# Splitting w_down in three stages instead of two: a new spread of 64 pieces, with ScalarE issuing the output projection's stores

## The chip, the cores and the metric

The kernel runs on one NeuronCore of one Trainium2 chip. The metric is the device time of one execution in microseconds (us); lower is better. The engines are TensorE (PE in the profile, its weight loads PEld), VectorE (DVE), ScalarE (ACT), GpSimd (POOL) and SyncE (SP, which here only issues DMAs). SP and ScalarE each have a queue of DMAs of their own.

## What is computed

One layer of a hybrid decoder on 2048 prompt tokens and 8 sample tokens, width 1024, all float32:

```
proj = x @ w_in                        # columns: u (512), v (512), xs (512)
u = gelu(proj_u);  v = layer_norm(gelu(proj_v))
y_a = u * chunk_spatial_gate(v)        # 128x128 lower-triangular W_s per head, chunks of 128 tokens
y_b, state = s5_mixer(xs)              # diagonal complex state space layer, 32 groups, then gelu and GLU
x1 = layer_norm(2**0.25 * x + concat(y_a, y_b) @ w_out)
y  = layer_norm(2**0.25 * x1 + grouped_moe(x1))     # 16 experts, top 2; h @ w_down[e] per expert
```

TensorE multiplies rounded fp32r operands. To keep float32 accuracy each operand is split in a high part (rounded to fp32r) and a low part (the difference), and a product is made of three: high x high, high x low, low x high.

## The kernel before

The program is five stages with a barrier of all engines behind each (`phase()`). In the time of the profiled execution:

* **Input projection**, 0 to 270 us. 8 halves `i` of 256 tokens, 4 feature groups `f` each; a step is `n = 4 i + f`. TensorE turns the rows of x, and projects them to xs and u (L697). ScalarE rounds the turned x (`high`, L404), VectorE makes its low part (`low`, L478). From step `LATE` = 16 on, each step also builds the matrices of one pair of state groups: VectorE computes them (`v_pair`, L632 to L635), TensorE turns them (`pair_mats`, L715, L724), VectorE copies them out (`results`, L642). VectorE's order in a late step is `v_pair`, `xs_tile` (L491), `low` in even steps, `results`. ScalarE's is `u_tile` (L416), then `high` in even steps. GpSimd builds other matrices beside it (L373 to L389).
* **v projection**, 270 to 391 us. 16 tiles `c` of 128 tokens. TensorE multiplies (L1087; the gate's product L1065 for tile c - 3), ScalarE applies gelu (L920), VectorE normalises tile c + 4 and gates tile c (`norm_tile`, `gate_tile`) and fills cosine and sine tables between them (`table_step`); at c = 6 it also does the sample tokens. The turned x comes back from DRAM in 8 parts of two tiles, in two buffers: `half(i)` on SP's queue (L862) once the product of tile 2 i - 3 is done. At the end SP issues the first loads of the next stage (L805 to L807) when the tables are finished (`tables_set`, L1050).
* **State space layer**, 391 to 519 us.
* **Output projection**, 519 to 789 us. 17 tiles `p` (tile 0 is the sample). ScalarE rounds the mixer's output of tile p + 2 (`high`, L1655), GpSimd makes the low part (`low`, L1591) and behind it, in its own order, the inverse root for the layer norm of tile p (`root`, L1596); TensorE multiplies (L1831), turns x1 (L1842) and does the router's product (L1851). VectorE's order is `norm(p + 1)`, `turn(p)`, `units(p)`, and every second tile `select` (the experts' choice, L1717 on). Its `norm` needs GpSimd's root (L1776), so ScalarE's `high` stands ahead of it.
* **Experts**, 789 to 1352 us.

**The split of w_down.** w_down is 64 pieces of 128 x 512 ("units"). Each is loaded from the input to SBUF, ScalarE writes its high part, VectorE its low part, and both parts are stored to DRAM, 256 KB each, from where the experts' stage loads them. This rides along with other stages. Before, 24 units are split in the input projection and 40 in the output projection. In the input projection the list `UNITS` gives step and place of each unit: SP loads at step n (L298), ScalarE rounds at n + 1 behind `u_tile` and ahead of `high` (L420), VectorE subtracts at n + 2 (L495), SP stores at n + 3 (L291). In the output projection `STEPS_D[p]` has the units of tile p. SP loads them behind the layer norm of tile p (L1559), ScalarE rounds them in `units(p)` (L1688) at the end of tile p and thus ahead of its `high(p + 3)`, VectorE subtracts them (L1791), and SP stores them in its turn for tile p + 1 (`units_out`, L1565), behind the loads and stores of that tile. There SP may load the units of tile p only when the stores of tile p - 2 have landed.

Of the kernel before, what the change touches and what calls it, by code (L numbers as in the profile page):

```python
# [6 lines left out]
P = 128  # L7
# [23 lines left out]
SUP = 512  # L31
# [66 lines left out]
def hybrid_step(nc, a, o):  # L98
    ctx = ExitStack()
    with ctx, nc.allow_non_contiguous_dma(reason="small parameters are laid out by state"):  # L100
# [93 lines left out]
        with phase() as ph:  # L194
# [22 lines left out]
            LIFE = 4  # L217
            UNITS, busy = [], {}
            for n in range(6, 27):
                free = [s for s in SLOTS if busy.get(s, 0) <= n and n + LIFE <= SLOTS[s]]  # L220
                free.sort(key=lambda s: SLOTS[s])
                for s in free[:1 + n % 2]:
                    if len(UNITS) < 24:
                        UNITS.append((n, s))
                        busy[s] = n + LIFE
            AUNITS = len(UNITS)
            assert AUNITS == 24, AUNITS
            wd_ld, wd_st = ({s: phase_sem(f"wd_{k}_{s}") for s in SLOTS} for k in ("in", "stored"))
            wd_high, wd_low = sems("a_wd_high a_wd_low")

            def units_at(n):
                return [(j, s, sum(u[1] == s for u in UNITS[:j])) for j, (m, s) in enumerate(UNITS) if m == n]

# [19 lines left out]
            def _(sp):  # L253
# [33 lines left out]
                def units(n):  # L287
                    for j, s, m in units_at(n - 3):
                        sp.wait_ge(wd_low, j + 1)
                        for h in range(2):  # L290
                            sp.dma_start(wd_dram[h][j // 4, :, j % 4 * SUP:(j % 4 + 1) * SUP],  # L291
                                         wd_part(s, 1 - h, True).bitcast(F32)).then_inc(wd_st[s], 16)
                    for j, s, m in units_at(n):
                        if m:
                            sp.wait_ge(wd_st[s], m * 32)
                        elif s[0] == "x":
                            sp.wait_ge(turned[int(s[1])], 1)
                        sp.dma_start(wd_part(s, 0, False), wd_src[j // 4, :, j % 4]).then_inc(wd_ld[s], 16)  # L298
# [97 lines left out]
            def _(act):  # L396
# [15 lines left out]
                def u_tile(i, f):  # L412
                    act.wait_ge(u_prod, i * FT + f + 1)
                    if f == 0 and f"y{i}" in SLOTS:
                        act.wait_ge(wd_st[f"y{i}"], uses(f"y{i}") * 32)
                    nc.scalar.activation(ya[:, 2 * i:2 * i + 2, f, :], pu[f % 2][:, 0:XH].rearrange("p (t n) -> p t n", n=P),  # L416
                                         ACT.Gelu_apprx_tanh).then_inc(u_out, 1)
                    for j, s, m in units_at(i * FT + f - 1):
                        act.wait_ge(wd_ld[s], m * 16 + 16)
                        nc.scalar.copy(wd_part(s, 1, True), wd_part(s, 0, False)).then_inc(wd_high, 1)  # L420
# [47 lines left out]
            def _(dve):  # L468
# [18 lines left out]
                def xs_tile(i, f):  # L487
                    dve.wait_ge(xs_prod, i * FT + f + 1)
                    if i % 2 == 0 and i:
                        dve.wait_ge(ust_stored[f], i // 2 * 16)  # L490
                    v.tensor_copy(ust[:, f, :, i % 2 * (KS // 2):(i % 2 + 1) * (KS // 2)].rearrange("p j k -> p k j"),  # L491
                                  pxs[f % 2][:, 0:XH].rearrange("p (k j) -> p k j", j=L)).then_inc(xs_out, 1)
                    for j, s, m in units_at(i * FT + f - 2):
                        dve.wait_ge(wd_high, j + 1)
                        v.tensor_tensor(wd_part(s, 0, True), wd_part(s, 0, False), wd_part(s, 1, True).bitcast(F32),  # L495
                                        ALU.subtract).then_inc(wd_low, 1)
# [312 lines left out]
        with phase() as ph:  # L809
# [44 lines left out]
            LAG = 3  # L854
            SMP = 10
            block = ph.enter_context(nc.Block())

            @block.sync
            def _(sp):
# [18 lines left out]
                for j in range(L):  # L878
                    sp.dma_start(toep[:, j, :], k_dram[(L - 1 - j) * Q:(L - 1 - j) * Q + P, :]).then_inc(toep_in, 16)
                for i in range(2, NH):  # L880
                    sp.wait_ge(v_prod, 2 * i - 2)
                    half(i)
                sp.wait_ge(vs_set, 1)
# [31 lines left out]
            def _(act):  # L915
# [12 lines left out]
                nc.scalar.activation(vs[:], psv[:, :], ACT.Gelu_apprx_tanh).then_inc(vs_gelu, 1)  # L928
                with act.Fori(1, CH // 4 - 1) as i:
                    for b in range(4):  # L930
                        gelu(i * 4 + b, b, False)
                for b in range(4):
                    gelu(CH - 4 + b, b, False)

            @block.vector
            def _(dve):
# [106 lines left out]
                for c in range(CH - 4):  # L1043
                    gate_tile(c, c % 4)
                    if c < len(rest):
                        table_step(*rest[c])
                    norm_tile(c + 4, c % 4)
                    if c + 4 == SMP:
                        sample()
                v.memset(tw[:, 3], 0.0).then_inc(tables_set, 1)  # L1050
                for c in range(CH - 4, CH):
# [411 lines left out]
        with phase() as ph:  # L1463
# [40 lines left out]
            wd_high, wd_low = sems("d_wd_high d_wd_low")  # L1504
            STEPS_D, used, left = {}, {}, NUNITS - AUNITS
            for p in range(2, CH):
                free = [t for t in range(p) if used.get(t, 0) <= p - 2][:min(3 + (p in (8, 12)), left)]
                STEPS_D[p] = [(NUNITS - left + k, t) for k, t in enumerate(free)]
# [17 lines left out]
            def _(sp):  # L1526
# [33 lines left out]

                def units_out(p):
                    sp.wait_ge(wd_low, landed(p, 1, 1))
                    for u, t in STEPS_D[p]:
                        for h in range(2):
                            sp.dma_start(wd_dram[h][u // 4, :, u % 4 * SUP:(u % 4 + 1) * SUP],  # L1565
                                         (yb_r, ya_r)[h][:, t].bitcast(F32)).then_inc(wd_st[p % 2], 16)

                for p in range(2, CH + 1):
# [5 lines left out]
                    stores(p, p % 2)  # L1574
                    if p - 1 in STEPS_D:
                        units_out(p - 1)
                for b in range(2):
                    sp.wait_ge(wd_st[b], landed(CH - 2 + b, 2, 32))
                for s in (x1_stored, ax1_stored):
# [69 lines left out]
            def _(act):  # L1649
# [33 lines left out]
                act.wait_ge(sc_zero, 1)  # L1683
                score(0, NS)
                def units(p):
                    act.wait_ge(wd_ld[p % 2], landed(p, 2, 16))
                    for u, t in STEPS_D[p]:
# [13 lines left out]
            def _(dve):  # L1701
# [83 lines left out]
                for k in range(KD):  # L1785
                    dve.wait_ge(wo_high, k + 1)
                    v.tensor_tensor(wo[1][:, k, :], w_out[:, k, :], wo[0][:, k, :].bitcast(F32), ALU.subtract).then_inc(wo_low, 1)
                def units(p):
                    dve.wait_ge(wd_high, landed(p, 1, 1))
                    for u, t in STEPS_D[p]:  # L1790
# [23 lines left out]
                turn(CH - 1, 1)  # L1814
                units(CH - 1)
                norm(CH, 0, False, CH // 2)
# [644 lines left out]
```

## Time and profile before

| | |
|---|---|
| time, median of 3 runs | 1350.77 us (1349.82 to 1352.14) |
| the profiled execution | 1353.23 us, span 1351.6 us |
| TensorE busy | 1193.4 us, 88% |
| VectorE busy | 924.0 us, 68% |
| ScalarE busy | 513.0 us, 38% |
| GpSimd busy | 479.3 us, 35% |
| DMA | 290 MB, mean 215 GB/s |
| granted TensorE clock, mean | 0.943 of full speed |

The span is from the first to the last instruction; the execution's own time is 1.6 us more. The busy shares are averages over stages with different limits, so each stage has to be read by itself: which engine works without a pause in it, and which wait ends last. Of a busy time only the part that nothing else covers is in the total.

### The profile page before, as it was taken

Reading aid. Unit: us, or ns where it says so; the run is one execution under the profiler, and the core shown is the slowest. Engines: PE = TensorE matmul, PEld = TensorE weight load, DVE = VectorE, ACT = ScalarE, POOL = GpSimd, SP = SyncE. Lnnn points to the kernel's source line nnn. Section 1 sums busy time; section 2 is a strip of 40 time slices with the busy share of each in tenths; the row PEclk is TensorE's granted clock in tenths of the full one; section 3 lists DMA queues with packets and bytes.
Section 4 is the critical chain, followed back from the end, with each engine's and each line's share of the span. In section 5 each row is a group of like instructions: output and inputs, shape, how many; then the busy total and the mean of one; then the engine's idle time right before and its main releaser. Section 6 shows DMA issues by size and latency. Waiting matters only on the chain. (4 is left out here: it accounts for less than half of the span.)

```text
span 1351.6 us, 23750 instructions
## 1 busy us (share of the span) xinstructions
PE 1193.4 (88%) x7005; PEld 1014.3 (75%) x7006; DVE 924.0 (68%) x2044; ACT 513.0 (38%) x808; POOL 479.3 (35%) x552
## 2 busy tenths in 40 slices
PE   7999889799978977999999668999999999999910
PEld 6997889778867744888887567888888888888800
DVE  3463875558877745457777686877787778777685
ACT  4131111100003254223223224666666666666533
POOL 3108860100010003322222023555554555454467
PEclk9999899999989988999989778999999999999965
DMA  8589684674335332457877774899989889745594
GB/s 257 166 311 289 190 267 136 180 222 170 126 104 160 116 130 57 155 187 262 270 268 256 257 288 165 265 288 317 278 274 297 246 255 303 218 95 121 123 348 171
DMA packets 142833, 290.04 MB, mean 215 GB/s; under 512 B 54632, under 2 KB 71608, under 8 KB 131472
## 3 DMA queue, kind: packets, MB, share of 16 engines
q1 hardware_dynamic: 126320, 231.99, 50.2%
q0 software_dynamic: 15408, 55.12, 17.4%
q10 hardware_dynamic: 1040, 2.10, 0.5%
q8 instruction: 37, 0.61, 0.2%
q14 instruction: 28, 0.23, 0.1%
HBM read 177.90 MB, written 111.13 MB: 214 GB/s over the span
## 5 line engine op out<-in xcount | busy, mean ns | idle before, releaser
L2174 DVE TENSOR_TENSOR wgu<-w_raw,wgu (+1 forms) x192 | 229.9, 1220 | 83.4 <-ACT wgu L2270 82.6
L2391 PE MATMUL p_gu<-wgu,xg_high 128*128 x768 | 246.4, 402 | 8.3 <-DVE xg_low L2167 4.5
L2270 ACT CAST wgu<-w_raw x188 | 192.6, 1051 | 55.3 <-issue 52.3
L2391 PEld LDWEIGHTS p_gu<-wgu,xg_high 128*128 128x128 f32 x768 | 141.4, 190 | 42.4 <-issue 15.1
L2391 PE MATMUL p_gu<-wgu,xg_low 128*128 x384 | 152.0, 396 | 0.0
L2053 POOL TENSOR_TENSOR spare_e<-nothing 128x1 f32<-128x1 f32 x48 | 46.4, 966 | 219.0 <-DVE yo L2193 219.0
L2054 POOL DMA_INDIRECT acc_rows<-yo,si x48 | 112.3, 2340 | 8.7 <-issue 8.7
L1831 PE MATMUL p_out<-w_out_high,mixt_high 128*128 128x512 f32 x256 | 103.4, 404 | 0.0
L1831 PE MATMUL p_out<-w_out_high,mixt_low 128*128 128x512 f32 x256 | 101.5, 396 | 0.0
L1831 PE MATMUL p_out<-w_out_low,mixt_high 128*128 128x512 f32 x256 | 101.3, 396 | 0.0
L2391 PEld LDWEIGHTS p_gu<-wgu,xg_low 128*128 128x128 f32 x384 | 72.8, 190 | 15.8
L2415 PE MATMUL p_d<-wd_high,ht_high 128*128 x192 | 80.1, 417 | 1.3 <-DVE ht_low L2187 1.3
L697 PE MATMUL pxs<-xt_high,w_xs_high 128*128 128x256 f32 x256 | 77.7, 303 | 2.7 <-DVE xt_low L478 2.0
L1591 POOL TENSOR_TENSOR mixt_low<-ya,mixt_high 128x512 fp32r<-128x512 f32 x16 | 22.8, 1426 | 155.2 <-ACT mixt_high L1655 155.2
L2415 PE MATMUL p_d<-wd_high,ht_low 128*128 x192 | 75.9, 395 | 0.0
L2415 PE MATMUL p_d<-wd_low,ht_high 128*128 x192 | 75.7, 394 | 0.0
L697 PE MATMUL pxs<-xt_high,w_xs_low 128*128 128x256 f32 x256 | 75.1, 294 | 0.0
L697 PE MATMUL pxs<-xt_low,w_xs_high 128*128 128x256 f32 x256 | 75.1, 293 | 0.0
L2167 DVE TENSOR_TENSOR xg_low<-p_xt,xg_high 128x512 fp32r<-128x512 f32 x96 | 61.8, 685 | 16.4 <-ACT xg_high L2257 15.8
L697 PE MATMUL pu<-xt_high,w_u_high 128*128 128x256 f32 x256 | 72.5, 283 | 0.0
L697 PE MATMUL pu<-xt_high,w_u_low 128*128 128x256 f32 x256 | 72.4, 283 | 0.0
L697 PE MATMUL pu<-xt_low,w_u_high 128*128 128x256 f32 x256 | 72.4, 283 | 0.0
(453 smaller groups left out, 2902.3 us busy)
## 6 DMA issues: line engine op xcount, KB each, us to landing
w_raw<-in_w_gate SPq DMA_DIRECT2D x16, 1024.0 KB, 7.4
w_raw<-in_w_up SPq DMA_DIRECT2D x16, 1024.0 KB, 10.3
wd_high<-w_down_high SPq DMA_DIRECT2D x16, 1024.0 KB, 6.9
wd_low<-w_down_low SPq DMA_DIRECT2D x16, 1024.0 KB, 9.5
ya_u<-in_w_down SPq DMA_DIRECT2D x54, 256.0 KB, 4.3
w_down_low<-ya_r SPq DMA_DIRECT2D x54, 256.0 KB, 6.6
w_down_high<-yb_r SPq DMA_DIRECT2D x40, 256.0 KB, 7.6
acc_rows<-ax SPq DMA_DIRECT2D x18, 512.0 KB, 7.6
```

What stands on the lines that cost most here:

```text
L697: mm = t.matmul(banks[f % 2][:, 0:XH], (w_hi, w_lo)[h][w][:, k, f * P:(f + 1) * P], xt[x][:, i % 2, k, :], start=(k == 0 and x + h == 0), ...
L1591: gp.tensor_tensor(mixt[1][:, b, part, 0:n], src, mixt[0][:, b, part, 0:n].bitcast(F32), ALU.subtract).then_inc(mix_low, 1)
L1831: mm = t.matmul(po[b][m][0:n, :], mixt[x][:, b, k, 0:n], wo[w][:, k, m * SUP:(m + 1) * SUP], start=(k == 0 and x + w == 0), stop=(k == KD ...
L2053: gp.tensor_tensor(spare[:], nothing[:], nothing[:], ALU.add)
L2054: gp.indirect_dma_start(acc_dram, bass.IndirectOffsetOnAxis(ap=si[:, b:b + 1], axis=0), yo[:, b, :], None, compute_op=ALU.add).then_inc(ad ...
L2167: low = tt(xl[:, b, part, :], pt_x[h], xh[:, b, part, :].bitcast(F32), ALU.subtract)
L2174: low = tt(wgu[:, slot, 1, at], raw[:, slot, at], wgu[:, slot, 0, at].bitcast(F32), ALU.subtract)
L2270: nc.scalar.copy(wgu[:, slot, 0, at], raw[:, slot, at]).then_inc(hi_set, 1)
L2391: mm = t.matmul(pg[b][:, :, :], x[:, b, k, :], w[h][:, k], start=(k == 0 and x is xh and h == 0), stop=(k == KD - 1 and x is xl))
L2415: mm = t.matmul(pd[m][:, :], ht[x][:, b, k, :], w[h][:, k, m * SUP:(m + 1) * SUP], start=(k == 0 and x + h == 0), stop=(k == 1 and x == 1))
```

## The change

The 64 units are spread anew over three stages: 18 in the input projection, 12 in the v projection, 34 in the output projection.

* Input projection: the first 12 units stay. The last 12, which ScalarE rounded in steps 16 to 26, become 6, loaded at steps 17, 18, 20, 21, 23 and 25. For a unit loaded at step 16 or later, rounding, subtraction and store are one step later than before: n + 2, n + 3, n + 4.
* v projection: 12 units, one per tile. ScalarE rounds unit c behind the gelu of tile c + 4, VectorE subtracts it behind `norm_tile(c + 4)`. SP's queue now serves, for each c, `half` (every second c), the stores of unit c - 4 (which wait for VectorE's subtraction) and the load of unit c - 2, in this order; it waits for the last stores ahead of the loads for the next stage. ScalarE's loop of four tiles is written out.
* Output projection: units in tiles 2 to 13 only (2 1 3 2 3 3 4 3 4 3 3 3, before 2 1 3 2 3 3 4 3 3 3 4 3 3 3 in tiles 2 to 15). The stores are issued by ScalarE, at the end of its tile p for the units of tile p - 1, ahead of its rounding of the units of tile p.

```diff
-            UNITS, busy = [], {}
-            for n in range(6, 27):
...
+            UNITS = [(6, "y4"), (7, "y5"), (7, "y6"), (8, "y7"), (9, "x2"), (9, "x3"), (10, "y4"), (11, "y5"), (11, "y6"), (12, "y7"), (13, "x2"), (13, "x3"),
+                     (17, "y6"), (18, "x2"), (20, "x3"), (21, "y7"), (23, "x2"), (25, "x3")]
...
-            def units_at(n):
-                return [(j, s, sum(u[1] == s for u in UNITS[:j])) for j, (m, s) in enumerate(UNITS) if m == n]
+            def units_at(n, after=0):
+                return [(j, s, sum(u[1] == s for u in UNITS[:j])) for j, (m, s) in enumerate(UNITS)
+                        if m + (after and after + (m >= LATE)) == n]
...
-                    for j, s, m in units_at(n - 3):
+                    for j, s, m in units_at(n, 3):
...
-                    for j, s, m in units_at(i * FT + f - 1):
+                    for j, s, m in units_at(i * FT + f, 1):
...
-                    for j, s, m in units_at(i * FT + f - 2):
+                    for j, s, m in units_at(i * FT + f, 2):
...
+            BUNITS = 12
...
-                for i in range(2, NH):
-                    sp.wait_ge(v_prod, 2 * i - 2)
-                    half(i)
+                def unit_out(j):
+                    sp.wait_ge(wd_low, j + 1)
+                    u = AUNITS + j
+                    for h, part in enumerate((wd_hi[j % 3], wd_lo[j % 3])):
+                        sp.dma_start(wd_dram[h][u // 4, :, u % 4 * SUP:(u % 4 + 1) * SUP], part[:].bitcast(F32)).then_inc(wd_st[j % 3], 16)
+
+                def unit_in(j):
+                    if j >= 3:
+                        sp.wait_ge(wd_st[j % 3], j // 3 * 32)
+                    u = AUNITS + j
+                    sp.dma_start(wd_raw[j % 3][:], wd_src[u // 4, :, u % 4]).then_inc(wd_ld[j % 3], 16)
+
+                for c in range(2, BUNITS + 4):
+                    sp.wait_ge(v_prod, c)
+                    if c % 2 == 0 and c // 2 + 1 < NH:
+                        half(c // 2 + 1)
+                    if c >= 4:
+                        unit_out(c - 4)
+                    if c < BUNITS + 2:
+                        unit_in(c - 2)
+                for s in range(3):
+                    sp.wait_ge(wd_st[s], BUNITS // 3 * 32)
...
-                with act.Fori(1, CH // 4 - 1) as i:
-                    for b in range(4):
-                        gelu(i * 4 + b, b, False)
-                for b in range(4):
-                    gelu(CH - 4 + b, b, False)
+                for c in range(4, CH):
+                    gelu(c, c % 4, False)
+                    if c - 4 < BUNITS:
+                        act.wait_ge(wd_ld[(c - 4) % 3], (c - 4) // 3 * 16 + 16)
+                        nc.scalar.copy(wd_hi[(c - 4) % 3][:], wd_raw[(c - 4) % 3][:]).then_inc(wd_high, 1)
...
+                    if c < BUNITS:
+                        dve.wait_ge(wd_high, c + 1)
+                        v.tensor_tensor(wd_lo[c % 3][:], wd_raw[c % 3][:], wd_hi[c % 3][:].bitcast(F32), ALU.subtract).then_inc(wd_low, 1)
...
-            STEPS_D, used, left = {}, {}, NUNITS - AUNITS
-            for p in range(2, CH):
-                free = [t for t in range(p) if used.get(t, 0) <= p - 2][:min(3 + (p in (8, 12)), left)]
+            FIRST_D = AUNITS + BUNITS
+            STEPS_D, used, left = {}, {}, NUNITS - FIRST_D
+            for p in range(2, 13 + 1):
+                free = [t for t in range(p) if used.get(t, 0) <= p - 2][:min(4 if p in (8, 10) else 3, left)]
...
-                    if p - 1 in STEPS_D:
-                        units_out(p - 1)
...
+                def units_out(p):
+                    act.wait_ge(wd_low, landed(p, 1, 1))
+                    for u, t in STEPS_D[p]:
+                        for h in range(2):
+                            act.dma_start(wd_dram[h][u // 4, :, u % 4 * SUP:(u % 4 + 1) * SUP],
+                                          (yb_r, ya_r)[h][:, t].bitcast(F32)).then_inc(wd_st[p % 2], 16)
+
                 def units(p):
+                    if p - 1 in STEPS_D:
+                        units_out(p - 1)
+                    if p not in STEPS_D:
+                        return
                     act.wait_ge(wd_ld[p % 2], landed(p, 2, 16))
```

## Rows read from the trace of the kernel before

**Rows 1.** By stretch: length, busy PE, PEld, DVE, ACT, POOL; clock, DMA share, GB/s.
```profile
128.00:252.00 124.00, 114.99 (x920) 114.11 (x920) 85.95 (x163) 18.11 (x37) 57.51 (x83) 0.94 0.67 201
...
270.00:391.00 121.00, 113.51 (x546) 92.86 (x546) 91.55 (x356) 10.50 (x18) 10.45 (x21) 0.97 0.45 153
...
760.00:789.00 29.00, 7.86 (x43) 7.24 (x43) 14.76 (x48) 3.74 (x8) 1.68 (x2) 0.55 0.61 199
```
**Rows 2.** Instructions in order of time: start, us, [idle before <- releaser]; around 150 and 200 us.
```profile
153.81 1.27 ACT L420 CAST xin_r<-xin 128x512 fp32r<-128x512 f32 x2 [2.54 <-DMA xin<-in_w_down]
155.59 1.29 DVE L478 TENSOR_TENSOR xt_low<-tp,xt_high 128x512 fp32r<-128x512 f32 x2 [3.22 <-ACT xt_high L404]
161.90 0.33 PE L715 MATMUL pst<-ident,v_re 128*128 128x128 f32 x1 [3.10 <-DVE v_im L635]
...
199.90 0.47 PE L715 MATMUL pst<-ident,v_re 128*128 128x128 f32 x1 [4.05 <-DVE v_im L635]
```
**Rows 3.** Waits of 128 to 252 us: total, times, longest.
```profile
PE pst L715 <- DVE v_im L635: 8.3, 4, 4.1
```
**Rows 4.** Busy time by stretch, where the clock was low.
```profile
162.00:169.00 7.00, 7.00 (x34) 7.00 (x35) 6.97 (x11) 0.00 (x0) 6.24 (x9) 0.51 0.61 175
199.70:206.50 6.80, 6.60 (x31) 6.60 (x32) 4.70 (x12) 0.00 (x0) 0.00 (x0) 0.50 0.80 195
```
**Rows 5.** Line L495: duration ns min/median/max, first and last start.
```profile
L495 DVE TENSOR_TENSOR xin_r<-xin,xin_r x10: 674/692/1228, 91.5 to 232.3; 128x512 fp32r<-128x512 f32 x10
```
**Rows 6.** VectorE's waits of 300 to 391 us, the longest and the third.
```profile
DVE vn L996 <- POOL rs L906: 8.6, 13, 0.7
...
DVE k_lag L1007 <- PE pg L1065: 0.5, 1, 0.5
```
**Rows 7.** VectorE, TensorE and SP in order of time, 352 to 391 us.
```profile
352.13 0.32 SPq L862 DMA_DIRECT2D xt_high<-x_turned_high  x1
...
364.30 1.12 DVE L1007 SCALAR_TENSOR_TENSOR k_lag<-pg,g_col,bs_row 128x128 f32<-128x128 f32 x4
...
367.30 0.48 PE L1087 MATMUL pv<-wv_high,xt_high 128*128 128x512 f32 x1
...
382.54 0.07 DVE L1050 MEMSET tw<- 128x16 f32 x1
...
382.68 2.66 SPq L805 DMA_DIRECT2D umat<-u_blocks  x4
...
390.08 0.60 SPq L807 DMA_DIRECT2D sq<-sq_mats  x1
```
**Rows 8.** Lines L862, then L291: us from issue to landing.
```profile
DMA to landing us min/median/max: 4.7/6.1/7.4
...
DMA to landing us min/median/max: 2.7/4.6/7.8
```
**Rows 9.** In order of time, the end of the output projection.
```profile
758.32 1.85 PE L1851 MATMUL p_router<-w_r,x1t 128*128 128x16 f32 x16
...
763.40 1.66 ACT L1688 CAST yb_r<-ya_u 128x512 fp32r<-128x512 f32 x3 [3.02 <-DMA ya_u<-in_w_down]
765.09 1.90 DVE L1791 TENSOR_TENSOR ya_r<-ya_u,yb_r 128x512 fp32r<-128x512 f32 x3 [5.85 <-ACT yb_r L1688]
766.91 1.28 DVE L1761 SCALAR_TENSOR_TENSOR z<-z,p_out 128x512 f32<-128x512 f32 x2
...
775.85 3.57 PE L1851 MATMUL p_router<-w_r,x1t 128*128 128x16 f32 x16 [0.83 <-ACT x1t L1665]
```
**Rows 10.** Lines L1565 and L456: duration ns of the issue, min/median/max.
```profile
L1565 SPq DMA_DIRECT2D w_down_high<-yb_r x40: 452/769/1475, 578.9 to 777.3; - x40
...
L456 ACTq DMA_DIRECT2D w_v<-in_w_in x1: 434/434/434, 250.0 to 250.0; - x1
```
**Rows 11.** Waits of 535 to 790 us (ScalarE) and 645 to 740 us (VectorE).
```profile
ACT yb_r L1688 <- DMA ya_u<-in_w_down: 25.0, 9, 4.1
...
DVE x L1776 <- POOL rs L1596: 24.0, 7, 8.3
```

More of the change, by code:

```diff
@@ L217, in hybrid_step @@
             LIFE = 4
-            UNITS, busy = [], {}
-            for n in range(6, 27):
[L220 to L225, printed above, removed]
+            UNITS = [(6, "y4"), (7, "y5"), (7, "y6"), (8, "y7"), (9, "x2"), (9, "x3"), (10, "y4"), (11, "y5"), (11, "y6"), (12, "y7"), (13, "x2"), (13, "x3"),
+                     (17, "y6"), (18, "x2"), (20, "x3"), (21, "y7"), (23, "x2"), (25, "x3")]
+            for s in SLOTS:
+                steps = [n for n, u in UNITS if u == s]
+                assert all(n - m >= LIFE + (m >= LATE) for m, n in zip(steps, steps[1:] + [SLOTS[s]]))
             AUNITS = len(UNITS)
-            assert AUNITS == 24, AUNITS
             wd_ld, wd_st = ({s: phase_sem(f"wd_{k}_{s}") for s in SLOTS} for k in ("in", "stored"))
             wd_high, wd_low = sems("a_wd_high a_wd_low")
-            def units_at(n):
-                return [(j, s, sum(u[1] == s for u in UNITS[:j])) for j, (m, s) in enumerate(UNITS) if m == n]
+            def units_at(n, after=0):
+                return [(j, s, sum(u[1] == s for u in UNITS[:j])) for j, (m, s) in enumerate(UNITS)
+                        if m + (after and after + (m >= LATE)) == n]
             def uses(s):
@@ L855, in hybrid_step @@
             SMP = 10
+            BUNITS = 12
+            u_at = Place(nc, base + 116 * KB)
+            wd_raw = [sb(f"wd_raw{s}", [P, SUP], where=Place(nc, u_at.at + s * 4 * KB)) for s in range(3)]
+            wd_lo = [sb(f"wd_lo{s}", [P, SUP], F32R, where=Place(nc, u_at.at + s * 4 * KB)) for s in range(3)]
+            wd_hi = [sb(f"wd_hi{s}", [P, SUP], F32R, where=Place(nc, u_at.at + s * 4 * KB + 2 * KB)) for s in range(3)]
+            assert pl.at <= u_at.at
+            wd_ld, wd_st = ([phase_sem(f"b_wd_{k}{s}") for s in range(3)] for k in ("in", "stored"))
+            wd_high, wd_low = sems("b_wd_high b_wd_low")
             block = ph.enter_context(nc.Block())
@@ L1559, in units_in @@
                         sp.dma_start(ya_u[:, t], wd_src[u // 4, :, u % 4]).then_inc(wd_ld[p % 2], 16)
[L1561 to L1566, printed above, removed]
                 for p in range(2, CH + 1):
@@ L1574, in _ @@
                     stores(p, p % 2)
-                    if p - 1 in STEPS_D:
-                        units_out(p - 1)
                 for b in range(2):
-                    sp.wait_ge(wd_st[b], landed(CH - 2 + b, 2, 32))
+                    sp.wait_ge(wd_st[b], landed(CH + b, 2, 32))
                 for s in (x1_stored, ax1_stored):
@@ L1788, in units @@
                 def units(p):
+                    if p not in STEPS_D:
+                        return
                     dve.wait_ge(wd_high, landed(p, 1, 1))
@@ L1814, in _ @@
                 turn(CH - 1, 1)
-                units(CH - 1)
                 norm(CH, 0, False, CH // 2)
```

## The prediction, made before the changed kernel was run

> **What bounds the kernel now.** I read the table of busy time by stretch first, then the waits of each stretch, then the engines side by side in order of time where a wait is long. TensorE is the busiest engine over the span, but the reader should see in [rows 1] that the three stages which the change touches have different limits.
>
> In the late steps of the input projection TensorE is busy for 115.0 of 124 us at a clock of 0.94. It waits four times for VectorE's `v_im`, 8.3 us in all [rows 3], of which two waits are long, 3.10 and 4.05 us [rows 2]. The first can be followed back: TensorE's product at 161.90 waited for VectorE, whose `low` at 155.59 had been idle for 3.22 us behind ScalarE's `high`, and ScalarE had stood 2.54 us at 153.81 until a loaded unit landed. So a unit's load, asked for one step too late, stops TensorE some 8 us later. Right behind each of the two waits the granted clock is at its lower level, 1.2 GHz, for about 7 us [rows 4].
>
> In the v projection it is VectorE that has no pause. Its busy time, 91.6 of 121 us, hides that: of 300 to 391 us its waits are 13 round trips to GpSimd of 0.7 us at most, which stand inside every norm, and hardly more [rows 6]. Each further instruction there lengthens the stage. The stage's end has a second chain of the same length: SP may issue the next stage's loads only when VectorE has finished its tables at 382.54, and takes from 382.68 to 390.68 for them [rows 7]; the barrier falls at 391.
>
> In the output projection TensorE and VectorE are both nearly full until 760. Behind that stands a tail of 29 us with TensorE busy for 7.9 of it at a clock of 0.55 [rows 1]: the last tile's norm, turn, router and choice in series.
>
> **Input projection: -13.5 us.** Six of twelve late units go and the other six are rounded two steps behind their load. A step is about 7 us of TensorE, the loads landed 2 to 3 us too late [rows 2], so no rounding waits for a load any more and `high` follows its turn at once. The two long waits go, 3.10 + 4.05 = 7.15 us. The low clock went with them: 7.0 us at 0.51 and 6.8 us at 0.50 [rows 4] cost half their length, 6.9 us. Together 14.0. What is late next is `v_pair` itself, which the two short waits (8.3 - 7.15 = 1.1 us) show already; these stay. The last unit's subtraction, 0.69 us [rows 5], now falls in step 28, where TensorE's steps are shortest, and I charge 0.5. Bounds: -8 if one drop of the clock comes anyway and a few short waits grow, -15 if the short ones go too.
>
> **v projection: +19.8 us.** I build it from four terms.
> * VectorE gets 12 subtractions. One is 0.69 us on its own [rows 5] and overlaps its neighbour by 0.08, so 0.61 each, 7.3 us in all, with nothing to hide them [rows 6]. ScalarE's 12 roundings lie beside TensorE's products, since ScalarE is busy for only 10.5 us of the stage [rows 1], and cost nothing.
> * SP's queue gets a wait. The stores of unit c - 4 wait for a subtraction that VectorE makes at the end of its turn c - 4, and `half` of the next c is queued behind it. VectorE runs behind TensorE: the last `half` was issued at 352.13, but VectorE ended turn 7 only at 364.30 [rows 7]. With eight units more it ends it at 364.3 + 8 x 0.61 = 369.2. Two stores and a load are issued (1.3), then the last `half`. Its two transfers take 7.4 us at most, the second issued 0.4 later [rows 8], and they now stand behind 0.75 MB of units, an estimated 1.5 us: landed at 379.8, though the product that needs it began at 367.30. Two products and a gate, 12.0 us, then gelu, norm and subtraction, 3.6, end VectorE's turn 11 at 395.4. VectorE's own work alone would end it at 382.5 + 7.3 = 389.8. So 5.6 us.
> * The last stores (0.9 us to issue, 4.6 to land, [rows 8]) now stand ahead of the 8.0 us of loads for the next stage: 5.5 us. Before, these loads ended together with VectorE, so nothing covers it.
> * TensorE waits some 6 us for the last `half`, longer than the waits behind which the clock was low in [rows 4]. If the clock is low for the next two products, that costs up to 3.4 us; I take 1.4.
>
> Low bound +12.8: the first and third term alone, with the parts landing in time. High bound +24: the full 3.4 and 2 us more for landings.
>
> **Output projection: -7.3 us.** Tiles 14 and 15 have no units. The last product ended at 758.3, but the last norm started at 766.91: ScalarE waited until 763.40 for the units of tile 15, VectorE 5.85 us for ScalarE, then subtracted three [rows 9]. Now the norm starts when the product ends, about 758.5, and the choice ahead of it has 2.5 us of slack more from tile 14. That gives 8.4, and all of the tail follows. The last routers ran at the low clock, 3.57 us against 1.85 for the same form [rows 9]; with the pause ahead of them cut from 10.6 to about 2 us, I count half of the difference, 0.9. Up to tile 13 as many units are split as before, 34, so VectorE's work there is the same.
>
> Against it, ScalarE issues 68 stores. [rows 10] give 0.43 us for the one DMA that ScalarE issues now, and 0.77 for SP's issue of these stores: 29.5 or 52.3 us. They stand ahead of the roundings, and the queue behind them is `high`, GpSimd's `low`, GpSimd's root, and the norm, which VectorE waited for in 7 of the tiles from 645 to 740, 24.0 us in all [rows 11]. What covers the stores is the time in which ScalarE waits for loads anyway, 25.0 us in 9 tiles [rows 11], of which about 6 belong to tiles 14 and 15. At 0.43 some 10 us stay uncovered. Half of them fall in tiles before 8, where the chain has room, and of the other half about 2 us are left after the slack of the six late tiles. At 0.77 half of 33 falls there, and some 13 us would show. I take 2, nearest to ScalarE's own row. Loads of tile p also wait for stores of tile p - 2, issued at about the time at which SP issued them; I charge nothing.
>
> **Sum.** -13.5 + 19.8 - 7.3 = -1.0 us. The profiled execution took 1353.2 us with 1.6 us around its span, so it would become 1352.2; that execution lies 2.4 above the median of the three runs, 1350.8, and on their scale the forecast is 1349.8. About 0.2%, 2.7 us, is what a measurement can tell from no change here. So I forecast no change, made of three large terms that cancel.
>
> **The rivals.**
> *The v projection hides more than I think.* If SP's stores of a unit come soon enough for the parts to land in time, its cost is +12.8 and the sum -8.0: 1342.8. For it speaks that TensorE has two tiles, 12.7 us, between the release and the need of a part. Against it, VectorE is 12 us behind at turn 7.
> *ScalarE as issuer becomes the limit (the slower side).* Place: ScalarE's 6 to 8 stores per tile, ahead of `high`. Price: +10 instead of +2 in tiles 8 to 13, so 1350.8 + 7.0 = 1357.8. It decides from about 0.7 us an issue on, where eight stores take 5.6 us and no wait for a load, 4.1 at the longest [rows 11], covers them. For it speaks SP's 0.77 under the same traffic. Against it, SP's slow issues stood behind 2.5 MB of its own transfers, and ScalarE's queue has only the stores. On this the Trainium skill, "DMA: Bandwidth & Descriptors", section "Issuing engines are not separate DMA queues", says that DMAs of all issuing engines share the same 16 DMA engines and that a second issuer saves only issue time. By that rule the traffic that slowed SP's issue is there for ScalarE too, and the sum would be that of this rival, +7; by the row of ScalarE's own issue it is -1.
> *The input projection keeps its waits.* VectorE's `v_pair` runs beside GpSimd's work, and a short wait grows in place of the long ones, with the clock falling behind it. Then it gives -6 and the sum is +6.5: 1357.3. For it speaks that two short waits are there now; against it, they were 1.1 us together and the clock stayed up behind them.
> *The change does not do what it says*: the stores or waits turn out as before. I see no way for it, since the steps are fixed lists.
>
> **Chances.** The forecast with its three terms 0.40, the first rival 0.25, ScalarE as issuer 0.20, the input projection 0.13, anything else 0.02. The forecast's own range is 1344 to 1355. The range over the cases is 1340 to 1360. Faster by over 0.2% is the first rival and the lower part of the forecast's range, 0.39; within 0.2% 0.27; slower 0.34.
>
> **What would show it.** Right: no rounding of a unit between 128 and 240 waits for a DMA, TensorE's waits for `v_im` are under 2 us in all, the clock stays up there, and the stage ends some 13 us sooner. In the v projection the products of tiles 8, 10, 12 and 14 wait for the loaded parts, the last for about 6 us, and the stage is 19 to 20 us longer, with some 5 us on SP between the last subtraction and the next stage's loads. From the last product of the output projection to its end it is 8 to 9 us less, and ScalarE's issue is near 0.45 us. Wrong: the v projection grows by under 14 us, the late tiles of the output projection by over 5, or a clock drop remains between 128 and 252.

## The result, and the profile after

The changed kernel takes 1363.29 us (median of 13 runs, 1353.62 to 1366.78) against 1351.21 us (13 runs, 1347.27 to 1353.74): ratio 1.0089, 95% interval 1.0075 to 1.0104. It is 12 us slower, where 1349.8 and a range of 1340 to 1360 were forecast. The profiled execution has a span of 1363.0 us.

Cut at the places that the rows name, the two profiled executions differ so. The products of the output projection are those of its tiles 1 to 16 (L1862, before L1831); the sample's, tile 0, stand ahead of them in the third row.

| us | before | after | difference | forecast |
|---|---|---|---|---|
| input projection, to the first product of the v projection | 270.05 | 256.52 | -13.5 | -13.5 |
| v projection, to the next stage's first load | 112.63 | 136.79 | +24.2 | +19.8 |
| from there to the output projection's first product | 150.16 | 149.65 | -0.5 | 0 |
| its products, first to last | 225.64 | 234.27 | +8.6 | +2 |
| from there to the last choice | 28.98 | 21.16 | -7.8 | -9.3 |
| experts | 564.16 | 564.60 | +0.4 | 0 |

The first row came out to a tenth, the tail behind the last product within 1.5 us. Two terms went wrong: the v projection by 4.4 us and the products of the output projection by 6.6.

By stretch the changed kernel shows the late steps of the input projection, the v projection, and the tail (columns as in [rows 1]):

```profile
128.00:238.50 110.50, 108.84 (x920) 108.17 (x921) 84.15 (x157) 14.65 (x31) 56.97 (x84) 1.00 0.59 180
256.50:402.00 145.50, 119.31 (x546) 96.96 (x546) 98.85 (x368) 16.82 (x30) 10.44 (x21) 0.89 0.60 192
778.70:800.00 21.30, 9.20 (x43) 8.57 (x44) 12.08 (x44) 2.19 (x5) 1.68 (x2) 0.52 0.12 49
```

TensorE's 920 products of the late steps took 124 us before [rows 1] and take 110.5 now, at a clock of 1.00 instead of 0.94. The v projection's same 546 stand in 145.5 us instead of 121, with the clock down to 0.89. In the tail the clock is no better than it was.

TensorE's waits in the input projection, the answer to [rows 3]:

```profile
PE pst L712 <- DVE v_im L632: 1.0, 1, 1.0
```

And in the v projection, from 270 to 392 us, first the row of the kernel before, where TensorE waited twice for VectorE and never for a part, then the two of the changed kernel:

```profile
PE pg L1065 <- DVE ya L1011: 4.4, 2, 2.8
...
PE pv L1114 <- DMA xt_low<-x_turned_low: 16.1, 3, 8.2
...
PE pg L1092 <- DVE ya L1035: 3.2, 1, 3.2
```

The chain behind the longest wait for a part, in order of time, TensorE, SP and VectorE, the answer to [rows 7]:

```profile
358.63 0.32 SPq L889 DMA_DIRECT2D w_down_high<-wd_hi  x1
...
359.97 0.45 SPq L867 DMA_DIRECT2D xt_high<-x_turned_high  x1
...
370.86 0.76 PE L1114 MATMUL pv<-wv_high,xt_high 128*128 128x512 f32 x1 [8.22 <-DMA xt_low<-x_turned_low]
...
380.10 0.69 DVE L1014 BATCH_NORM_STATS2 st<-vg 128x6 f32<-128x512 f32 x1 [8.36 <-ACT vg L944]
...
389.33 0.07 DVE L1077 MEMSET tw<- 128x16 f32 x1
389.81 0.43 SPq L889 DMA_DIRECT2D w_down_low<-wd_lo  x1
393.31 2.67 SPq L802 DMA_DIRECT2D umat<-u_blocks  x4
```

SP stands at the store of piece 7 until VectorE's turn 7 is over, only then asks for the last part of the turned x, at 359.97, and TensorE has it at 370.86. The first product behind the wait takes 0.76 us instead of 0.48: the clock is low, 0.57 from 370.8 to 378 us. VectorE, which had no pause in [rows 6], now waits 8.36 us, and the tables end at 389.33. SP then waits once more, from 390.24 to 392.9, for the last stores, issues a small store, and comes to the next stage's loads at 393.31. A part takes longer to land than in [rows 8]:

```profile
  PE pv L1114: 16.1, 3
...
DMA to landing us min/median/max: 5.0/8.4/11.3
```

In the output projection ScalarE issues at these durations (ns, min/median/max), the answer to [rows 10]:

```profile
L1708 ACTq DMA_DIRECT2D w_down_high<-yb_r x34: 326/483/1170, 594.4 to 767.2; - x34
L1708 ACTq DMA_DIRECT2D w_down_low<-ya_r x34: 326/586/1430, 594.8 to 768.1; - x34
```

One tile of it, ScalarE and VectorE in order of time:

```profile
715.57 0.18 ACT L1689 ACTIVATE scores<-p_router 128x16 f32<-128x16 f32 x1 [1.11 <-PE p_router L1882]
715.58 0.33 ACTq L1708 DMA_DIRECT2D w_down_high<-yb_r  x1
...
720.01 0.58 ACTq L1708 DMA_DIRECT2D w_down_low<-ya_r  x1
720.63 1.66 ACT L1718 CAST yb_r<-ya_u 128x512 fp32r<-128x512 f32 x3 [4.87 <-issue]
722.20 0.62 ACT L1674 CAST mixt_high<-ya 128x512 fp32r<-128x512 f32 x1
...
727.20 1.28 DVE L1806 SCALAR_TENSOR_TENSOR x<-z,rs,b_row 128x1024 f32<-128x1024 f32 x1 [3.01 <-POOL rs L1615]
```

Eight stores take from 715.58 to 720.6 us. The loads of this tile were asked for at 710.62 and had landed at 716.7, so the rounding waits for nothing else ("issue"), and `high`, GpSimd and the norm are late behind it. ScalarE's and VectorE's waits over the output projection follow, from 535 to 790 us, ScalarE's against its row in [rows 11]. For VectorE [rows 11] has a shorter stretch, so its row of before over the whole stage stands first:

```profile
DVE x L1776 <- POOL rs L1596: 42.3, 17, 8.3
...
ACT yb_r L1718 <- issue: 26.7, 7, 4.9
ACT yb_r L1718 <- DMA ya_u<-in_w_down: 10.3, 4, 3.5
...
DVE x L1806 <- POOL rs L1615: 56.7, 17, 8.6
```

The 10.3 us that are put down to loads are issue time too: in all eleven tiles that round behind stores, the rounding starts within 0.05 us of the end of the last issue, and the loads have landed before it.

### The profile page after: what moved, and what is told of

Same layout as the page of the kernel before. It is cut to its first block and busy times, and to the rows that moved or that the text cites. A ratio compares the mean times of both kernels' runs of the same rounds, so it can differ in the third digit from the quotient of the medians.

```text
span 1363.0 us, 23746 instructions
## 1 busy us (share of the span) xinstructions
PE 1196.9 (88%) x7005; PEld 1016.4 (75%) x7006; DVE 925.0 (68%) x2044; ACT 513.4 (38%) x808; POOL 478.6 (35%) x552
## 5 line engine op out<-in xcount | busy, mean ns | idle before, releaser
L1862 PE MATMUL p_out<-w_out_high,mixt_high 128*128 128x512 f32 x256 | 104.1, 407 | 0.0
L1862 PE MATMUL p_out<-w_out_high,mixt_low 128*128 128x512 f32 x256 | 102.0, 398 | 0.0
L1862 PE MATMUL p_out<-w_out_low,mixt_high 128*128 128x512 f32 x256 | 101.9, 398 | 0.0
L1114 PE MATMUL pv<-wv_high,xt_high 128*128 128x512 f32 x128 | 54.7, 427 | 23.4 <-DMA xt_low<-x_turned_low 16.1
L413 ACT ACTIVATE ya<-pu 128x256 f32<-128x256 f32 x32 | 12.2, 383 | 164.5 <-PE pu L694 164.5
```

Of the source, the lines that this page charges most:

```text
L1114: mm = t.matmul(pv[c % 2][:, :], lhs, wv[w][:, k, :], start=(k == 0 and x + w == 0), stop=(k == KD - 1 and x == 1))
L1862: mm = t.matmul(po[b][m][0:n, :], mixt[x][:, b, k, 0:n], wo[w][:, k, m * SUP:(m + 1) * SUP], start=(k == 0 and x + w == 0), stop=(k == KD ...
```

## The experiments

Each was timed in five rounds beside the kernel before, which took 1350.5 to 1350.9 us there and 1351.2 beside the changed kernel. A difference from the changed kernel's median is therefore up to 0.7 us too large, and the intervals reach some 2 to 3 us to either side. The stages are those of the profiled executions; "v and state" runs from the first product of the v projection to the first of the output projection's tile 1.

| kernel | median us (runs) | ratio, 95% interval | input | v and state | products | tail |
|---|---|---|---|---|---|---|
| before | 1351.21 (13) | 1 | 270.1 | 262.8 | 225.6 | 29.0 |
| changed | 1363.29 (13) | 1.0089 (1.0075 to 1.0104) | 256.5 | 286.4 | 234.3 | 21.2 |
| e1, no pieces in the v projection | 1337.72 (5) | 0.9902 (0.9882 to 0.9921) | 256.9 | 263.0 | 233.4 | 20.7 |
| e2, stores on SP | 1351.73 (12) | 1.0013 (0.9998 to 1.0028) | 257.3 | 286.9 | 223.1 | 21.2 |
| e3, parts on ScalarE | 1351.55 (12) | 1.0008 (0.9995 to 1.0021) | 256.3 | 275.5 | 236.5 | 20.7 |
| e4, loads before the wait | 1362.01 (6) | 1.0079 (1.0060 to 1.0098) | 257.6 | 283.4 | 235.9 | 20.7 |
| e5, e2 + e3 + e4 | 1337.53 (6) | 0.9895 (0.9874 to 0.9916) | 256.5 | 271.9 | 222.9 | 20.7 |
| e6, e5 and GpSimd subtracts | 1342.49 (6) | 0.9931 (0.9912 to 0.9951) | 257.4 | 276.1 | 223.1 | 20.7 |
| e7, half of the stores on ScalarE | 1352.16 (12) | 1.0009 (0.9990 to 1.0027) | 256.6 | 284.7 | 225.8 | 20.7 |
| e8, no later step | 1370.56 (5) | 1.0146 (1.0124 to 1.0169) | 264.9 | 286.6 | 231.1 | 21.2 |
| e9, e6 placed behind the norm | 1339.01 (5) | 0.9918 (0.9905 to 0.9932) | 257.0 | 269.2 | 223.6 | 21.2 |
| e10, 6 and 40 pieces, else e5 | 1346.24 (12) | 0.9965 (0.9952 to 0.9977) | 256.2 | 268.6 | 239.6 | 20.7 |

One execution of each was profiled, and stages that no edit touched show the scatter. The input projection took 256.2 to 257.6 us in the ten kernels with the same list, and the v and state stages 284.7 to 286.9 us in the four that have them as changed. The products took 231.1 to 236.5 us in the five kernels in which ScalarE issues all stores of 34 pieces, and 222.9 to 223.6 us in the four in which SP issues them. These last two groups stand clear of each other; a difference of 1 to 2 us between two stages does not.

**e1: what the 12 pieces cost in the v projection.** Their load, rounding, subtraction and stores are taken out there, and the last stage reads others in their place:

```diff
-                        sp.dma_start(wd[h][...], wd_dram[h][expert(e)])
+                        sp.dma_start(wd[h][...], wd_dram[h][expert(e) - 4 * (4 <= expert(e) < 8)])
```

> The changed kernel without the 12 pieces of the v projection: none is loaded, rounded, subtracted or stored there, and experts 4 to 7 load the pieces of experts 0 to 3. The work on these 12 pieces is left out. Theory (the v projection costs what its stretch grew by, 24 us, and nothing of it is given back later): 1363.3 - 24 = 1339 us, products of the v projection end 19.9 us sooner, loads of the next stage begin 24 us sooner. Rival (part of the growth would be there anyway, from the input projection's end or is made good in the state space stage): over 1345.

25.6 us less, near the 24 expected. The stage is back at its length before, 263.0, and nothing is given back behind it.

**e2: who issues the output projection's stores.** `units_out(p - 1)` goes from the head of ScalarE's `units(p)` to SP's turn of tile p, behind `stores(p)`:

```diff
-                    if p - 1 in STEPS_D:
-                        units_out(p - 1)      # ScalarE, ahead of the roundings
...
                     stores(p, p % 2)
+                    if p - 1 in STEPS_D:
+                        units_out(p - 1)      # SP
```

> The changed kernel with the output projection's stores back on SP's queue, in SP's turn of tile p + 1, everything else as changed. Theory (ScalarE's issue, 68 at 0.6 us, stands ahead of its roundings and high): the 17 products take 8 us less from first to last (226 instead of 234), in all 1363.3 - 8 = 1355; ScalarE's waits for loads come back to about 19 us. Rival 1 (the loads of tile p wait for late stores on either queue): within 2 us of the changed kernel. Rival 2 (only the granted clock differs): products in no stretch wait less, the low stretches only fall elsewhere.

11.6 us less, where 8 were expected, and the products take 223.1 instead of 234.3 us, 11.2 less. The clock is part of it, 0.98 against 0.95 over the products: TensorE is busy for 218.4 us instead of 225.0, and its pauses between products shrink by the other 4.6 us. So it is not the clock alone, and the norm's wait for GpSimd's root goes from 56.7 us to 40.4:

```profile
544.30:767.40 223.10, 218.37 (x1124) 184.82 (x1123) 152.21 (x386) 62.49 (x110) 58.49 (x62) 0.98 0.67 231
...
DVE x L1806 <- POOL rs L1624: 40.4, 17, 6.9
```

ScalarE's waits ahead of its roundings are now

```profile
ACT yb_r L1718 <- DMA ya_u<-in_w_down: 12.7, 5, 4.0
```

and not the expected 19: the loads have landed in most tiles when ScalarE comes to them. These waits are the cover that the forecast put at 19 us. Loads that wait for late stores are excluded as the changed kernel's loss: there each tile's loads are issued within 0.1 us of the norm that they follow. They did wait in the kernel before: SP issued those of tile 15 at 758.04, 9.8 us behind their norm, when the stores of tile 13 had landed (757.97).

**e7: half of them.** ScalarE issues the low parts' stores, SP the high parts':

```diff
-                        for h in range(2):
-                            act.dma_start(wd_dram[h][...], (yb_r, ya_r)[h][:, t]...)
+                        act.dma_start(wd_dram[1][...], ya_r[:, t]...)      # and wd_dram[0] by SP
```

> The changed kernel, but in the output projection only the low parts' stores (34) are issued by ScalarE, the high parts' 34 by SP in its turn of tile p + 1. Dose of the suspected cost: ScalarE's issue is halved, to some 21 us. Theory (each issue stands in the chain load, rounding, high, low, root, norm, and nothing covers it): half of the 11.6 us comes back, 1357.5. Rival (the first few issues per tile lie in ScalarE's wait for loads, only what goes beyond costs): three quarters or more come back, 1354 or less.

11.1 of the 11.6 us come back by the medians, and 8.5 of the 11.2 in the profiled products: the rival. ScalarE's waits fit it. In the seven tiles of the first row, two to four issues lie in the wait for the loads, and in the four of the second the issues outlast it:

```profile
ACT yb_r L1725 <- DMA ya_u<-in_w_down: 22.0, 7, 4.4
...
ACT yb_r L1725 <- issue: 6.0, 4, 2.9
```

**e3: the wait on SP ahead of the parts.**

```diff
-                    if c % 2 == 0 and c // 2 + 1 < NH:
-                        half(c // 2 + 1)      # SP, behind the stores of piece c - 5
...
                     nc.scalar.activation(vg[:, b, :], ...)
+                    i = (c + 1) // 2 + 1
+                    if c % 2 == 1 and i < NH:
+                        for n in range(2):
+                            act.dma_start(xv[n][:, i % 2]..., xt_dram[n][HALVES[i]])
```

> The changed kernel with the v projection's parts of the turned x (half) issued by ScalarE behind the gelu of tile 2 i - 3, so that they no longer stand behind SP's stores of pieces. Theory (SP's order: a wait for a subtraction ahead of the load): TensorE's three waits for the parts, 16.1 us, go, with the low clock behind them (5.0 us); VectorE's own work is what is left, 1363.3 - 13 = 1350. Rival (the parts are late since 768 KB of each piece share the DMA engines with them): issue is early but they land 8 to 10 us after it, and no more than 4 us is gained: 1359.

11.7 us less, 13 expected; the stage is 10.9 us shorter in the profile. No product waits for a part, though 256 KB in and 512 KB out per piece still share the DMA engines, so the rival falls. What TensorE waits for now is VectorE:

```profile
PE pg L1094 <- DVE ya L1037: 9.0, 2, 5.7
```

The tables end 119.1 us behind the first product, 6.6 more than before: the 12 subtractions.

**e4: the wait for the last stores.** `load` is cut in two, and the part of it that writes elsewhere goes ahead of the wait:

```diff
-                for s in range(3):
-                    sp.wait_ge(wd_st[s], BUNITS // 3 * 32)
...
                 for p in range(2):
-                    load(sp, p, p)
+                    load_u(sp, p, p)
+                for s in range(3):
+                    sp.wait_ge(wd_st[s], BUNITS // 3 * 32)
+                for p in range(2):
+                    load_sq(sp, p, p)
```

> The changed kernel, but at the end of the v projection SP issues the loads of the two pairs' inputs (16 DMAs of umat and us1, which lie elsewhere) before it waits for the last stores of the pieces, and the two matrices' loads behind. Theory (the wait stands alone on SP for 3.8 us with nothing beside it): 1363.3 - 3.8 = 1359.5, the barrier 3.8 us sooner. Rival (the first pair's products need what is loaded last anyway, or the issue itself slows beside the stores): within 1 us of the changed kernel.

The medians are only 1.3 us apart, 3.8 expected, and the intervals overlap. The stage is 3.0 us shorter in the profile, but 2.0 of them arise ahead of the edit's place: the tables already end 130.9 us behind the first product instead of 132.8. From the tables' end to the next stage's first product it is 11.7 us instead of 13.2, so the edit is worth about 1.5. SP reaches the first loads 2.6 us sooner, but the first product then waits 5.9 us for its matrix load, which is still issued behind the wait for the stores. This is the rival's first half.

**e8: the later step of the input projection.**

```diff
-                        if m + (after and after + (m >= LATE)) == n]
+                        if m + after == n]
```

> The changed kernel with its list of 6 late pieces in the input projection, but rounded, subtracted and stored at n + 1, n + 2, n + 3 again, as before the change. Theory (a load asked one step ahead lands 2 to 3 us late, and TensorE waits for v_im behind it): one or two long waits and a stretch of low clock come back, the first product of the v projection at 262 to 268 instead of 256.5, in all 1369 to 1375. Rival (six pieces fewer is what freed the steps, the later rounding adds nothing): within 2 us of the changed kernel.

7.3 us more, as the theory has it. With six pieces, but asked for one step ahead, two roundings wait for their load again. Behind the second of them VectorE's `low` stands 6.46 us and TensorE 6.13 us, the chain of [rows 2] once more. In order of time, ScalarE, VectorE, TensorE:

```profile
178.44 0.62 ACT L417 CAST xin_r<-xin 128x512 fp32r<-128x512 f32 x1 [4.47 <-DMA xin<-in_w_down]
...
187.40 0.62 ACT L417 CAST ya_r<-ya_u 128x512 fp32r<-128x512 f32 x1 [6.34 <-DMA ya_u<-in_w_down]
188.54 1.29 DVE L475 TENSOR_TENSOR xt_low<-tp,xt_high 128x512 fp32r<-128x512 f32 x2 [6.46 <-ACT xt_high L401]
...
194.72 0.47 PE L712 MATMUL pst<-ident,v_re 128*128 128x128 f32 x1 [6.13 <-DVE v_im L632]
```

So of the 13.5 us that the stage gained, 8.4 are the later step's, and 5.1 come with six pieces fewer even without it, each within the scatter of some 1 us.

**e5: the three edits together.**

> The three edits together: stores of the output projection on SP's queue, parts of the turned x issued by ScalarE in the v projection, loads of the next stage ahead of the wait for the last stores. Theory (three separate causes, one per stage or place, which add): 1363.3 - 11.6 - 11.8 - 1.3 = 1338.6, clear of the kernel before by 12. Rival (they overlap, or what one frees another wait takes): 1345 or more.

1337.53 us: 25.8 less than the changed kernel, as the sum of the three (24.6) says, and 1.05% faster than the kernel before (0.8% to 1.3%). The theory had 1338.6. The causes stand apart and add. This is the version to keep.

**e6 and e9: GpSimd instead of VectorE.** The subtraction of piece c - 4 moves into GpSimd's loop behind `root(c)`; e9 also waits for the norm:

```diff
+                    if 0 <= c - 4 < BUNITS:
+                        gp.wait_ge(wd_high, c - 3)
+                        gp.wait_ge(v_norm, c + 1)        # e9 alone
+                        gp.tensor_tensor(wd_lo[...], wd_raw[...], wd_hi[...], ALU.subtract).then_inc(wd_low, 1)
```

> As the three edits together, and in the v projection GpSimd instead of VectorE subtracts the 12 pieces, behind its root of tile c + 4. Theory (VectorE is the stage's limit, and GpSimd is busy there for 10.5 us of 121): the 12 x 0.61 = 7.3 us go, 1331.5. Rival (GpSimd's subtraction, 1.5 us or more, stands ahead of the next root or slows VectorE's instructions beside it): 0 to 3 us of gain, or a loss.

e6 is 5 us slower than e5, a loss as the rival allows. VectorE lost its subtraction, 0.69 us (7.3 us in all), but the last instruction of the norm, 0.55 us before, took 1.50 in 11 tiles (10.5 us in all; the mean over all its tiles is 1.3). In order of time, GpSimd and VectorE:

```profile
305.77 1.28 POOL L945 TENSOR_TENSOR wd_lo<-wd_raw,wd_hi 128x512 fp32r<-128x512 f32 x1
305.84 1.50 DVE L1033 TENSOR_SCALAR vn<-vg,ag,rs 128x512 f32<-128x512 f32 x1 [0.67 <-POOL rs L935]
307.26 1.11 DVE L1044 SCALAR_TENSOR_TENSOR k_lag<-pg,g_col,bs_row 128x128 f32<-128x128 f32 x4
308.41 0.69 DVE L1048 TENSOR_TENSOR ya<-k_lag,ya 128x512 f32<-128x512 f32 x1
```

> As GpSimd's subtractions with the three edits, but GpSimd also waits for VectorE's v_norm of tile c + 4, so that its 1.29 us lie beside VectorE's gate instructions (which read PSUM and one tensor of SBUF) and no longer beside the last instruction of the norm, which went from 0.55 to 1.31 us there. Theory (the two engines exclude each other in certain instructions only, and placement decides): the norm's instruction is back at 0.55 us; 7.3 us of subtractions are gone and up to 12 x 0.25 = 3 us come back at the product of u behind the gate: 1337.5 - 4.3 = 1333, at best 1330. Rival (GpSimd slows VectorE wherever it runs): 1337 or more, with longer gate instructions.

In e9 the same instructions read

```profile
304.50 0.55 DVE L1034 TENSOR_SCALAR vn<-vg,ag,rs 128x512 f32<-128x512 f32 x1 [0.67 <-POOL rs L935]
304.96 1.12 DVE L1045 SCALAR_TENSOR_TENSOR k_lag<-pg,g_col,bs_row 128x128 f32<-128x128 f32 x4
305.19 1.29 POOL L946 TENSOR_TENSOR wd_lo<-wd_raw,wd_hi 128x512 fp32r<-128x512 f32 x1 [0.73 <-DVE vn L1034]
306.11 0.91 DVE L1049 TENSOR_TENSOR ya<-k_lag,ya 128x512 f32<-128x512 f32 x1
```

The norm is back at 0.55 us, the gate's instructions beside GpSimd are as long as ever, and only the product behind them, which GpSimd's end still overlaps, takes 0.22 us more, as expected. So the theory of placement holds in its mechanism, and its time, 1333, was missed by 6 us. Placement brings no time that the runs can show: the profiled stage is 2.7 us shorter than in e5, the median 1.5 us above it, and e9's profiled execution was the fastest of its five. Its tables end 3.2 us sooner, but the first product of the next stage waits 7.2 us (6.2 in e5) for a matrix load issued behind the last stores.

**e10: where a piece is cheapest.**

```diff
-            BUNITS = 12
+            BUNITS = 6
...
-                free = [...][:min(4 if p in (8, 10) else 3, left)]
+                free = [...][:min(5 if p == 8 else 4, left)]
```

> The three edits together with another spread: 6 pieces in the v projection and 40 in the output projection (2 1 3 2 4 3 5 4 4 4 4 4 in tiles 2 to 13). Theory (after the three edits a piece costs VectorE's and ScalarE's time in either stage: (25.6 - 11.8 - 1.3) / 12 = 1.0 us each in the v projection, 0.6 + 0.6 in the output projection's chain): -6 and +7, within 2 us of 1337.5. Rival 1 (the output projection has room on SP's queue as it is): 1332. Rival 2 (loads of four and five pieces per tile land too late there, as the 40 pieces before did): 1343 or more.

8.7 us slower than e5: the theory, within 2 us of it, fails, and the second rival holds. In the profiled executions, of which e10's lies 3.5 us above its median, the six pieces fewer save 3.3 us in the v and state stages, and the products of the output projection take 239.6 us instead of 222.9. ScalarE's waits there, first e5's and then e10's, say why:

```profile
ACT yb_r L1727 <- DMA ya_u<-in_w_down: 11.2, 7, 2.7
...
ACT yb_r L1727 <- DMA ya_u<-in_w_down: 30.1, 8, 6.6
```

Part of the lateness is SP's: from tile 10 on it issues a tile's loads 1.3 to 2.7 us behind the norm. It may not issue them before the stores of tile p - 2 have landed, and two such landings, at 695.55 and 729.19, stand right ahead of the loads of tiles 11 and 13. In e5 the loads are at most 1.6 us behind.

## Why the prediction was wrong

* **Input projection, -13.5: right, and by its reason.** No rounding waits for a load, TensorE's waits for `v_im` are 1.0 us instead of 8.3, the clock is 1.00, and TensorE's products there are 6.2 us shorter in busy time, where 6.9 were forecast for the clock. e8 brings waits and low clock back by taking away the later step alone. That it came out to a tenth is luck, since the same stage scatters by 1.4 us.
* **v projection, subtractions, 7.3: right.** e3 leaves 6.6 us.
* **v projection, parts behind the stores, 5.6 + 1.4 = 7.0: the mechanism right, the size half.** It measured 13.7 us (tables' end of the changed kernel against e3's), 11.7 by the medians. The forecast followed the last part alone, as if VectorE worked without a pause until its turn 7. But TensorE waited for two earlier parts first, 3.3 and 4.5 us with low clock behind the second (0.57 from 332 to 340 us), and so turn 7 was itself late: SP's stores behind it were issued at 358.63, where the forecast's 369.2, less the 13.5 us of the stage before, is 355.7. And from these stores to the landing it reckoned 10.6 us (1.3 and 0.4 to issue, 7.4 for the longest landing of before, 1.5 for the pieces' traffic, an estimate for which no row gives a rate), where it took 12.1.
* **v projection, last stores, 5.5: 3.8** more than before between the tables' end and the first load. e4 confirms the place, and recovers 1.5 us of it.
* **Output projection, tail, -8.4: -7.8.** The last norm now starts 0.6 us behind the last product's end instead of 8.4 us, since VectorE is still at the choice ahead of it. The -0.9 for the routers did not come: the last took 3.56 us, as in [rows 9], for the shorter pauses, 1.55 and 0.83 us, did not keep the clock up.
* **Output projection, ScalarE as issuer, +2: this step failed.** It measured +8.6: 11.2 us that ScalarE's issuing costs (e2; 11.6 in the medians), less 2.6 us by which SP's version is faster than before in these tiles. The step took 0.43 us an issue from a single DMA, where 0.62 was measured over the 68 (42 us). Put into the forecast's own working, this makes 42 - 19 = 23 us uncovered, half of it in the late tiles, less the 3 us of slack that it took off: about +8. The other two terms of it do not hold either. The half in the tiles before 8 is not lost in slack: VectorE's norm of tile 8 ends 4.7 us late against the kernel before, and TensorE, whose products of tile 8 start 0.8 us late, starts those of tile 10 5.1 us late. And the cover was smaller: without the stores ScalarE waits for loads for 12.7 us (e2), not 19, and with them for none, since in every tile the issue outlasts the loads. This was the rival with a chance of 0.20; its price was +10, and its limit of 0.7 us an issue was too high, since at 0.62 it had come. e7 shows that the cost is not in proportion: half of the issues cost 2.8 us in the products (0.4 in the medians), all of them 11.2. The forecast had named the sign of it, the late tiles longer by over 5 us: from tile 8 on the products take 7.8 us more.

The sum with this rival alone was 1357.8; the parts' further 6.7 us, less 1.7 at the last stores, make 1362.8. That this meets 1363.3 is in part luck, as the rival's price is 1.4 us too high and the tail 1.5 us worse than forecast.

The forecast cited the Trainium skill, "DMA: Bandwidth & Descriptors", section "Issuing engines are not separate DMA queues", for the rule that a second issuer saves only issue time. For the stores the runs agree: SP's version loses nothing by issuing all of them, and what ScalarE's version spends is its own issue time. For the parts e3 shows more than the rule says, since a second issuer there saved 11.7 us, a wait in the first one's queue and not the time of its issues.

## What to carry to other kernels

Before a DMA is put on a compute engine's queue, count the issues per step at the duration that rows show under traffic, and compare them step by step with that engine's wait in the same step, not with the sum of its waits: what lies within the wait costs little (half of the stores, 2.8 us at most), what goes beyond it is in the chain (all of them, 11.2). When a queue gets a new wait, look at what is asked for behind it, follow the first late transfer and carry its delay to the next. Three costs in different places added up to within some 1 us here, so a slower result could be mended term by term.

## What the runs showed of the hardware

GpSimd's subtraction (two tensors of SBUF, 1.28 us) lengthens some of VectorE's instructions beside it and not others. TENSOR_SCALAR over 128x512 from SBUF to SBUF took 1.50 us instead of 0.55 in 11 tiles of e6, with its end 0.3 us behind GpSimd's. TENSOR_TENSOR with two tensors of SBUF took 0.91 us instead of 0.69 in e9 where it began 0.37 us before GpSimd's end. SCALAR_TENSOR_TENSOR with one tensor from PSUM and one from SBUF kept its 1.12 us beside it. The Trainium skill, "SBUF — State Buffer", section "Who interferes with whom", says that the two engines share a pair of ports under an exclusive lock. By that section `tensor_scalar` can enter a mode that uses both ports, `tensor_tensor` with both inputs in SBUF contends with GpSimd's reads, and an instruction with at most one SBUF input, outside such modes, does not contend. These traces agree in all three cases; they show durations, not the lock or the mode.

A DMA's issue on ScalarE took 0.33 to 1.43 us here, 0.62 from one to the next over the stage's products, with 220 GB/s of traffic; the one in a quiet stretch took 0.43 [rows 10].
